# The weight stream of a hybrid attention layer: two input chunks, then two compression chunks, in place of one and one

## The reference, cut to what matters

```
h = rms_norm(x, norm_w)
proj = h @ w_in                          # 2048 x 7704, split into 13 parts
k_cmp = silu(blocks(rope(k_c)) @ cmp_k_w1) @ cmp_k_w2    # w1: 4096 x 512
v_cmp = silu(blocks(v_c) @ cmp_v_w1) @ cmp_v_w2
o_a = g0 * attend(q, k_cmp, v_cmp) + g1 * selected(...) + g2 * window(...)
o_b = differential attention (two softmax maps, their difference, rms_norm per head)
x = x + concat(o_a * silu(z_a), o_b * silu(z_b)) @ w_out
return rms_norm(x, final_norm_w)
```

## Time and profile before

| | us |
|---|---|
| median of 3 runs | 515.6 |
| profiled execution | 515.5 |
| its span, first to last instruction | 513.3 |
| PE busy | 500.3 (97%) |
| DVE busy | 282.6 (55%) |
| ACT busy | 227.1 (44%) |
| mean DMA rate | 210 GB/s |

### The profile page before, as it was taken

The page is one execution under the profiler, slowest core; times in us unless marked ns, Lnnn a source line. Parts: engine busy times, 40 slices in busy tenths (PEclk is TensorE's granted clock), DMA queues, the critical chain, the costliest instruction groups (busy, mean ns, idle before and its releaser), DMA issues.

```text
span 513.3 us, 6145 instructions
## 1 busy us (share of the span) xinstructions
PE 500.3 (97%) x2454; PEld 406.0 (79%) x2454; DVE 282.6 (55%) x321; ACT 227.1 (44%) x311; POOL 45.2 (9%) x41
## 2 busy tenths in 40 slices
PE   7999999999999999999999999999999999999993
PEld 6788876667776788888888888888888878888882
DVE  3856813353443957676466647665545544644532
ACT  5847224233232644354644555464544353334231
POOL 1003300010010302010020000001000000113030
PEclk9999999999999999999999999999999999999998
DMA  8998449787778952444343444526864445455004
GB/s 275 412 420 303 163 165 343 282 313 290 305 282 312 348 213 98 165 155 147 109 140 111 160 163 153 185 83 222 332 266 165 170 177 202 189 174 222 14 1 163
DMA packets 17867, 107.69 MB, mean 210 GB/s; under 512 B 2224, under 2 KB 2736, under 8 KB 5936
## 3 DMA queue, kind: packets, MB, share of 16 engines
q1 hardware_dynamic: 16544, 104.86, 54.8%
q10 hardware_dynamic: 1296, 2.44, 1.4%
HBM read 105.20 MB, written 2.10 MB: 209 GB/s over the span
## 4 chain that ended last, share of the span: by engine, by line
PE 93%; issue 2%; DMA 1%; DVE 1%; SPq 1%; ACT 1%; POOLq 0%; POOL 0%; DVEq 0%
PE acc L962 25%; PE acc L964 24%; PE acc L963 24%; PE O L1002 3%; PE S L1104 3%; DMA raw<-stream 1%; PE S L1027 1%; PE S L1121 1%; PE acc L986 1%; PE acc L987 1%; PE acc L988 1%; PE S L1038 1%; PE S L1185 1%; PE S L964 1%; PE S L963 1%
## 5 line engine op out<-in xcount | busy, mean ns | idle before, releaser
L651 DVE TENSOR_TENSOR wlo<-raw,whi 128x2048 fp32r<-128x2048 f32 x72 | 166.4, 2313 | 184.6 <-ACT whi L388 184.4
L388 ACT ACTIVATE whi<-raw 128x2048 fp32r<-128x2048 f32 x72 | 138.1, 1918 | 171.5 <-PE acc L964 107.8
L962 PE MATMUL acc<-whi,hT_hi 128*128 128x512 f32 x432 | 172.6, 399 | 0.9 <-issue 0.9
L964 PE MATMUL acc<-whi,hT_lo 128*128 128x512 f32 x432 | 168.6, 390 | 0.0
L963 PE MATMUL acc<-wlo,hT_hi 128*128 128x512 f32 x432 | 168.3, 390 | 0.0
L962 PEld LDWEIGHTS acc<-whi,hT_hi 128*128 128x128 f32 x432 | 81.1, 188 | 29.4 <-issue 13.6
L964 PEld LDWEIGHTS acc<-whi,hT_lo 128*128 128x128 f32 x432 | 81.1, 188 | 17.4
L963 PEld LDWEIGHTS acc<-wlo,hT_hi 128*128 128x128 f32 x432 | 81.2, 188 | 15.8
L350 POOL TENSOR_TENSOR stage<-stage,stage 128x512 f32<-128x512 f32 (+1 forms) x16 | 25.0, 1574 | 193.1 <-DVE stage L694 193.1
L467 ACT ACTIVATE e<-S,small 128x128 f32<-128x128 f32 (+1 forms) x48 | 19.5, 419 | 26.1 <-DVE small L706 26.1
L962 PE MATMUL acc<-whi,mixA_hi 128*128 128x512 f32 x64 | 25.0, 391 | 0.0
(11 more groups left out here) (160 smaller groups left out, 491.2 us busy)
## 6 DMA issues: line engine op xcount, KB each, us to landing
raw<-stream SPq DMA_DIRECT2D x88, 1024.0 KB, 4.9
raw<-stream SPq DMA_DIRECT2D x6, 512.0 KB, 10.6
x_nat<-x_rows SPq DMA_DIRECT2D x2, 1024.0 KB, 13.1
x_nat<-x_rows SPq DMA_DIRECT2D x1, 2048.0 KB, 7.4
result<-x_nat SPq DMA_DIRECT2D x8, 256.0 KB, 3.2
xTs<-xT SPq DMA_DIRECT2D x3, 512.0 KB, 9.2
raw<-stream SPq DMA_DIRECT2D x4, 256.0 KB, 6.0
fw<-final_w ACTq DMA_DIRECT2D x1, 1024.0 KB, 5.3
```

The source lines that it names most:

```text
L388: act.activation(whi[:, n % SPLIT, :], raw[:, c % RAW, :], ACT.Copy).then_inc(hi_ready, 1)
L651: dve.tensor_tensor(wlo[:, n % SPLIT, :], raw[:, c % RAW, :], whi[:, n % SPLIT, :].bitcast(f32), ALU.subtract)\
L962: pe.matmul(acc_bank(n), xh, wh, start=k == 0, stop=False)
L964: last = pe.matmul(acc_bank(n), xl, wh, start=False, stop=k == KT - 1)
```

## The change

The interleaved part of the stream runs from place 9 to 40. Before, it has single chunks in turn: compression, input, compression, ..., with one place where two compression chunks follow each other. After, it has two of the input projection, two of the compression, eight times; the last compression chunk moves from place 39 to 40, the last one of the keys from 23 to 24. Steps at fixed places move with them: the gate products come at place 10 in place of 11 (behind the same chunk as before), the compressed keys one place later, the compressed values stay at place 42, and the second hidden layer's turn and SiLU go from places 40 and 41 to 41 and 42.

```diff
 STREAM = _in[:9]
-for _i in range(16):
-
-    STREAM += ([_in[9 + _i]] if _i < 2 else [_in[8 + _i]] if _i > 2 else []) + [_cmp[_i]]
-STREAM += _in[24:]
+for _i in range(0, 16, 2):
+
+    STREAM += _in[9 + _i:11 + _i] + _cmp[_i:_i + 2]
+STREAM += _in[25:]
@@
-GATE_AT = 11
+GATE_AT = 10
@@ scalar
-                if c == GATE_AT + 2:
+                if c == GATE_AT + 3:
                     act.wait_ge(g_turned, 1)
@@
-                if c == K_END + 4:
+                if c == K_END + 5:
                     act.wait_ge(cmp_out, 1)
@@ vector
-                if c == GATE_AT + 3:
+                if c == GATE_AT + 4:
                     dve.wait_ge(g_exp, TT)
@@ tensor
-                if c == GATE_AT + 1:
+                if c == GATE_AT + 2:
                     turn_gates()
                 if c == K_END + 1:
                     turn_hid(0)
-                if c == K_END + 3:
+                if c == K_END + 4:
                     cmp_keys()
                 if c == V_END + 1:
                     turn_hid(1)
-                if c == V_END + 3:
+                if c == V_END + 2:
                     cmp_values()
```

## The result

The changed kernel takes 517.58 us (median), the kernel before 515.85 in the same runs; the ratio is 1.0036, 95% interval 1.0024 to 1.0047. It is slower by 0.36%, and the interval lies above 1. The forecast was 515.3 within 514.0 to 516.6, a small gain: the sign is wrong, and the time lies outside the range. The profiled execution took 517.13 us for a span of 514.9, against 515.5 and 513.3 before. So 1.6 us are to be found. (One execution of the changed kernel was disturbed and took 1794.62 us; it is left out.)

The account below looks back on a forecast made before the run. PE, busy for 97% of the span, was taken to bound the kernel. First compressed scores at 186.34 instead of 186.68 gain 0.34: 515.5 becomes 515.2, plus 0.1 for the median, 515.3 us; range 514.0 to 516.6.

Parts of the forecast that it names:

- PE's own time: Interleaved stretch: two and two cost 13.07 us against 13.32 for two plain cycles, 0.25 less for each of seven pairs.
- The wait of the earlier trace: Near 86 us PE waited 0.95 us for a late input chunk before the change; foreseen to be gone.
- The transfers: At compression pairs, the input chunk third in a burst of four comes late: waits 0.13 and 0.58 us, 0.71 together.
- Rival C: Input chunk third in the burst lands late at every pair: waits 2.5 us, not 0.7; time 517.1 us; chance 0.14.
- The end of the stretch: Ahead of the first compressed scores PE waits 1.53 us for unit 0's exponentials, held behind chunk 43.
- rival A: Exponentials don't hold the compressed scores; PE arrives at 184.81, 1.87 us less, time 513.7 us; chance 0.14.
- the prediction's last sign of being wrong: The working as a whole is wrong if the end does not follow the start of the first compressed scores.
- The failed step: From the start of the first compressed scores on, all goes as before, so the gain is 0.34 us.
- three rivals: PE bound by itself, 513.7 us (chance 0.14); faster queue, 514.6 us (0.24); third chunks late, 517.1 us (0.14).

Follow-up runs that it names:

- first experiment: Changed kernel, with DVE taking the maxima of attention unit 0 ahead of the low half of chunk 43 instead of behind it: 513.65 us, ratio 0.9957.
- the filled stand: Changed kernel, with 26 idle matmuls on PE ahead of its wait for the exponentials of unit 0: 515.88 us, ratio 1.0005.
- the stand in the old kernel: Kernel before, with three idle subtractions on DVE ahead of the maxima of unit 0, making PE stand: 520.54 us, ratio 1.0078.
- the other edit: Maxima of unit 0 ahead of chunk 43's low half; on the changed kernel together with first input chunks issued first: 512.21 us, ratio 0.9928.
- the kernel with the input chunks first: Changed kernel, with SP issuing the first input chunk of each burst of four ahead of the two compression chunks: 515.55 us, ratio 0.9996.

## Why the prediction was wrong

Taken by its own steps, up to the point where it fails:

| | foreseen | measured |
|---|---|---|
| first compression chunk (C11) | 74.59 | 74.53 |
| C15 starts | 88.24 | 88.04 |
| I17 waits | 0.13 | 0 |
| I21 waits | 0.58 | 1.70 |
| C39 starts | 170.99 | 171.14 |
| chunk 43 lands | 176.85 | 177.16 |
| first compressed scores | 186.34 | 186.67 |
| PE stands there | 1.53 | 1.65 |
| from there to the second scores | as before (4.56) | 6.21 |
| time of the profiled execution | 515.2 | 517.13 |

**PE's own time: right, and a little better.** The wait of the earlier trace rows went. Two compression chunks take 1.86 us (88.04 to 89.90), not 1.98, which none of the rows could show, and the heads behind them 0.85 (foreseen 0.88). Over seven pairs this is 0.8 us. It happens to make up for the 1.0 us that the waits of the next point were longer than foreseen, so that the start of C39, 0.15 from the forecast, is right in part by luck.

**The transfers: the mechanism right, the size of one wait wrong.** Third chunks landed 9.78 (issue at 75.65, split at 85.43) to 11.18 us after the issue, the sum of the forecast was 10.29. The mean over the seven bursts is that as well; but I treated it as one number, and the wait depends on each. I21 had 11.11 us (89.17 to 100.28) and waited 1.70 in place of 0.58: 0.66 us because it was ready at 104.66 and not 104.00, the rest because PE came earlier. The other slow one (170.44) fell under the scores of unit 0. Rival C, all of them late, did not come. That its 517.1 is near the measured time is chance: its waits didn't occur, apart from the one at I21.

**The end of the stretch: right.** Chunk 43, its low half, the maxima, the exponentials, and PE 1.65 us early, 0.3 us from the clock time foreseen. The first experiment is close to rival A brought about by an edit. Its first scores at 184.64 and its 513.65 meet A's 184.81 and 513.7, so the rest of the sum holds. What happened in the changed kernel is the prediction's last sign of being wrong: the end did not follow the start of the first compressed scores.

**The failed step** is the sentence "After 186.34 the order is that of before, so the gain is 186.68 - 186.34 = 0.34". The order was that of before, the clock wasn't. I had priced the stand at its length and the work behind it at its old duration; what the stand does to the clock was put at nothing, without a reason. The first experiment (no stand, clock kept, 513.65), the filled stand (scores as late, clock kept in 8 of 11, 515.88) and the stand in the old kernel (520.54) show the missing term: 1.57 us in the profile, in 3 of 8 executions twice that by their time and mean clock. With it the same working gives 515.2 + 1.6 = 516.8, near the fastest of the executions. None of the three rivals held it, and so the range ended too low.

The changes of place of the gate's steps and the added table load cost PE nothing, as foreseen. The SiLU was done at 190.3 and PE asked for it at 194.6; the load stood between the split's end at 188.37 and the SiLU's start at 189.68, with no idle time beside its 1.28 us. The compressed keys come two places later, behind place 28 in place of 26, and not one as the section on the change says; PE does not wait there either. What stays open is what decides, from execution to execution, whether a stand lowers the clock and for how long; only the shares above are shown. Where the second step of the slowest executions lies is also open, since no profile shows one of the changed kernel. It isn't bound to the wait at chunk 21: the kernel with the input chunks first has no such wait in its profile, and four of its twelve executions show the step.

## What to carry to other kernels

When a plan makes a busy PE wait where it did not wait before, allow for a stretch at half clock behind it as well as for its length (1.6 us in most executions of the changed kernel, from nothing to some 3 us over all kernels here). Look for it in the granted clock of the windows after the wait, not in the waits. When a reordering moves a transfer, follow it to the first non-matmul work that stands behind it in an engine's order: here three lines on DVE brought 3.9 us (517.58 to 513.65). They turned a loss of 1.7 us by the pairing into a gain of 2.1, since the same lines on the kernel before gave 515.73. In a queue of mixed transfers, issue first what has the longest way to its use: here the split input chunks, not the compression chunks that PE reads as they are (2.0 us alone, 1.4 on top of the other edit).

## What was not expected of the hardware

A wait of 0.88 us (its length in one profile) lowered the clock in 5 of 12 executions. The half clock came about 2.5 us after PE had gone back to work in the changed kernel, and about 1.1 us after it in the old kernel with a made stand. Executions of one kernel fall into heaps some 1.3 to 1.7 us apart, each with its own mean clock. And two compression chunks behind each other take 1.86 us, 0.12 less than two alone.
